# Gate rows six steps earlier, output norm on VectorE alone, and scores led by a pair in the biased attention of a two-layer step

## The reference

```python
h = x * (1 + sc1) + sh1
y = mixer(h)                        # layer 1: grouped-query attention C, then neighbourhood attention D
x = layer_norm(DN_ALPHA * x + gt1 * y, g1, b1)
h = x * (1 + sc2) + sh2
x = layer_norm(DN_ALPHA * x + gt2 * peer_ffn(h), g2, b2)    # layer 1: this is the output y, z

# attention D, for the grid tokens (tiles 1, 2); the prompt tile has plain attention over itself
s_loc = q @ k * scale + bias[head, row offset, column offset]   # 256 local keys
s_loc = where(col_ok, s_loc, -inf)
s_ctx = q @ cached_k * scale                                    # 128 cached keys, no bias
out = softmax(concat(s_loc, s_ctx)) @ concat(v, cached_v)

# peer_ffn: 8 heads pick 16 of 16384 experts per token
out = sum(gate * gelu(u[expert] @ h) * v[expert])
```

## Time and profile before

| | us |
|---|---|
| runs: median (lowest to highest of 3) | 2543.14 (2542.46 to 2548.92) |
| profiled execution | 2539.47 |
| its span, first to last instruction | 2537.70 |
| TensorE busy in the span | 2362.0 (93%) |
| VectorE busy | 1765.0 (70%) |
| ScalarE busy | 772.8 (30%) |
| GpSimd busy | 915.0 (36%) |
| mean granted TensorE clock | 0.970 |

### The profile page before, as it was taken

One profiled execution on the slowest core, in us unless ns is written; L12 is line 12 of the kernel. 1 busy time (PEld: TensorE's weight loads), 2 busy tenths in 40 slices (PEclk: granted clock), 3 DMA queues, 4 the chain that ended last, 5 costly groups with the idle time before them and its releaser, 6 DMA issues.

```text
span 2537.7 us, 34148 instructions
## 1 busy us (share of the span) xinstructions
PE 2362.0 (93%) x12686; PEld 1819.5 (72%) x12686; DVE 1765.0 (70%) x3612; ACT 772.8 (30%) x1388; POOL 915.0 (36%) x650
## 2 busy tenths in 40 slices
PE   5988989999999999999978778999999999999994
PEld 4756789889757866666657467987995777666662
DVE  2335378978669877777644456799785897777775
ACT  2354442113225422222143444311330552222221
POOL 3500361621222265565353205335113124555551
PEclk7999989999999999999989988999999999999997
DMA  7445423986799899999834702279669999999992
GB/s 269 143 167 194 157 100 111 361 325 210 263 340 335 315 397 383 384 388 390 324 114 151 208 28 83 85 277 407 197 206 363 327 331 350 379 389 380 397 380 106
DMA packets 219907, 679.71 MB, mean 268 GB/s; under 512 B 32384, under 2 KB 63152, under 8 KB 219232
## 3 DMA queue, kind: packets, MB, share of 16 engines
q1 hardware_dynamic: 142912, 396.42, 43.7%
q0 software_dynamic: 76832, 281.11, 29.2%
HBM read 658.87 MB, written 18.56 MB: 267 GB/s over the span
## 4 chain that ended last, share of the span: by engine, by line
PE 83%; DMA 6%; DVE 5%; ACT 3%; issue 1%; SPq 1%; POOL 1%; ACTq 0%; DVEq 0%
PE ps L1056 21%; PE ps L1033 15%; PE ps L737 12%; PE ps L738 12%; PE ps L739 12%; DMA ring<-in_u 3%; PE ps L1012 2%; PE ps L900 2%; PE ps L919 2%; DVE v_split L2028 1%; PE ps L987 1%; PE ps L909 1%; PE ps L768 1%; PE ps L760 1%; DMA arena<-in_w_mod 1%
## 5 line engine op out<-in xcount | busy, mean ns | idle before, releaser
L655 POOL DMA_INDIRECT arena<-in_u_rows,arena x256 | 302.5, 1182 | 729.9 <-DVE arena L1844 549.7
L1056 PE MATMUL ps<-ring,arena 128*128 128x512 f32 x1264 | 564.9, 592 | 0.0
L1033 PE MATMUL ps<-arena,ring 128*128 128x256 f32 x2048 | 459.3, 382 | 11.2 <-DMA ring<-in_u 9.9
L655 POOL DMA_INDIRECT arena<-in_v,arena x256 | 354.2, 1384 | 319.2 <-DVE arena L1844 143.3
L1033 PEld LDWEIGHTS ps<-arena,ring 128*128 128x128 f32 x2048 | 384.2, 191 | 69.3 <-issue 18.7
L1056 PEld LDWEIGHTS ps<-ring,arena 128*128 128x128 f32 x1264 | 231.7, 190 | 241.9 <-issue 241.2
L1279 ACT ACTIVATE arena<-ps 128x256 f32<-128x256 f32 x256 | 98.1, 383 | 981.7 <-PE ps L739 618.5
L615 POOL TENSOR_TENSOR ring_lo<-ring,ring_hi 128x1024 fp32r<-128x1024 f32 x84 | 216.1, 2584 | 420.1 <-ACT ring_hi L1158 420.1
L737 PE MATMUL ps<-xs_high,u_split 128*128 128x256 f32 x1024 | 339.0, 331 | 0.0
L2057 DVE SCALAR_TENSOR_TENSOR arena<-arena 128x1024 f32<-128x1024 f32 x254 | 325.6, 1282 | 18.9 <-DMA arena<-in_v,arena 4.3
L1844 DVE CUSTOM_DVE_ANT_0 arena<-arena 128x1024 f32<-128x1024 f32 x256 | 311.0, 1220 | 15.3 <-DMA arena<-in_u_rows,arena 13.9
(11 more groups left out here) (245 smaller groups left out, 3565.2 us busy)
## 6 DMA issues: line engine op xcount, KB each, us to landing
ring<-in_u SPq DMA_DIRECT2D x256, 512.0 KB, 6.6
ring<-in_v SPq DMA_DIRECT2D x256, 512.0 KB, 5.7
ring<-in_w_mod SPq DMA_DIRECT2D x80, 512.0 KB, 4.3
ring<-in_w_in SPq DMA_DIRECT2D x36, 512.0 KB, 3.2
ring<-in_w_q SPq DMA_DIRECT2D x32, 512.0 KB, 3.2
gelu_half<-arena SPq DMA_DIRECT2D x120, 128.0 KB, 4.7
arena<-gelu_half SPq DMA_DIRECT2D x120, 128.0 KB, 4.6
arena<-in_w_mod SPq DMA_DIRECT2D x16, 512.0 KB, 19.5
```

Of the source, the lines that this page charges most:

```text
L655: pool.indirect_dma_start(row[at], None, table, bass.IndirectOffsetOnAxis(where[:, k:k + 1], axis=0)).then_inc(sem(f"row_in{at}"), 16)
L1033: ins = mm(hidden_bank(b), slot[c % RING][:, P * k:P * k + P], HFS[:, k, :], start=(k == 0), stop=(k == KC - 1))
L1056: ins = mm(ps[:, t + 3 * q, :], GL[:, b % GLS, P * t - P:P * t], slot[c % RING][:, 512 * q:512 * q + 512], start=(b == MIDDLE[0]), stop=(b ...
```

## The change

The gate rows go from steps 124-127 to 118-121 on TensorE and ScalarE, in both layers. The norm after the experts no longer waits for the whole last group with tile 1, but for its first four matmuls (a new semaphore). At the end of layer 0 VectorE does its half of tile 0's modulation between tile 1's residual and tile 1's factors; ScalarE does tile 1's normalize ahead of the split of the fourth weight chunk. At the end of layer 1 the whole norm is on VectorE: x minus mean times gain, then times the reciprocal root plus bias; ScalarE only takes the roots, and SyncE stores the tiles.

In the biased attention the bias table gets 384 columns per head, zero over the cached keys, and is held as eight times the bias plus mask, so that one instruction adds it to the raw scores, scales, writes the result and takes the maximum. Scores use four banks and are issued a pair ahead. The mask is added head by head in the last four steps of the attention before.

```diff
+GATE_ROWS = 118
...
+        def score_bank(l, g, i):
+            return (0, 1, 6, 7)[i % 4] if (l, g) == (1, 1) else i % 2
...
@@ SyncE, at its end @@
+            for t in range(NT):
+                sp.wait_ge(sem("y_ready"), t + 1)
+                sp.dma_start(a["y"][P * t:P * t + P, :], Xv[:, t, :]).then_inc(sem("y_out"), 16)
+            sp.wait_ge(sem("y_out"), 16 * NT)
...
@@ GpSimd, at its end @@
-            for t in range(NT - 1):
-                last_bias(t)
-            for t in range(NT):
-                wait_y(pool, t)
-                store(a["y"][P * t:P * t + P, :], Xv[:, t, :], "y_out")
-            pool.wait_ge(sem("y_out"), 16 * NT)
...
@@ TensorE, attention @@
+                lead = 1 if (l, g) == (1, 1) else 0
+                def scores(n):
+                    if n > lead:
+                        pe.wait_ge(sem("p_ready"), since("p_ready", 2 * l + g) + 2 * (n - lead))
+                    for i in (2 * n, 2 * n + 1):
...
+                        mm(ps[:, score_bank(l, g, i), 0:kn], QT[p0:p1, qn, P * t:P * t + P], KT[p0:p1, kt, k0:k0 + kn],
+                           start=True, stop=True).then_inc(sem("sc_ps"), 1)
+                for n in range(lead):
+                    scores(n)
                 for n in range(PAIRS + 2):
...
+                    if n + lead < PAIRS:
+                        scores(n + lead)
...
@@ TensorE, experts @@
+                        if b == KEYS - 1 and t == 1:
+                            ins.then_inc(sem("first_sums"), 1)
...
-                    m = b - KEYS + 4
-                    if m >= 0:
+                    m = b - GATE_ROWS
+                    if 0 <= m < 4:
...
@@ ScalarE @@
-                    m = b - KEYS + 4
-                    if m >= 0:
+                    m = b - GATE_ROWS
+                    if 0 <= m < 4:
                         gate_row(2 * l + 1, m, 0)
-                for c in range(start["uv", l] + 2 * KEYS - RING, start["uv", l] + 2 * KEYS - 2):
-                    done(c)
+                if l == 0:
+                    for c in range(start["uv", l] + 2 * KEYS - RING, start["uv", l] + 2 * KEYS - 2):
+                        done(c)
...
                     feature_half(n + 2, 0)
+                    normalize(n + 1, 1)
                     done(start["uv", l] + 2 * KEYS - 1)
-                    normalize(n + 1, 1)
                     feature_half(n + 2, 1)
...
                 else:
-                    normalize(n + 1, 1)
-                    normalize(n + 1, 2)
+                    for t in range(NT):
+                        deviation(n + 1, t)
...
@@ VectorE, norm @@
-                        if t:
+                        if t == 1:
+                            dve.wait_ge(sem("first_sums"), since("first_sums", n // 2) + 1)
+                        elif t == 2:
                             c = v_chunk(n // 2, KEYS - 1)
...
+                def scaled_rows(t):
+                    x = Xv[:, t, :]
+                    link(stt(x, x, mv[:, 2 * t:2 * t + 1], lnv[:, 0, :], ALU.subtract, ALU.mult))
+                    dve.wait_ge(sem("std"), since("std", n) + t + 1)
+                    link(dve.reciprocal(rstd[:, t:t + 1], rstd[:, t:t + 1]))
+                    stt(x, x, rstd[:, t:t + 1], lnv[:, 1, :], ALU.mult, ALU.add).then_inc(sem("y_ready"), 1)
                 if n < 3:
-                    factors(1)
-                    residual(2)
-                    factors(2)
+                    for t in range(NT):
+                        residual(t)
+                        if n == 1 and t == 1:
+                            features(2, 1)
+                        factors(t)
                 else:
...
+                    for t in range(NT):
+                        residual(t)
+                        dve.wait_ge(sem("var"), since("var", n) + t + 1)
+                        scaled_rows(t)
...
@@ VectorE, attention @@
-                bv = ar(A_BIAS, 4096).rearrange("p (n c) -> p n c", c=64)
-                link(tt(bv, bv, TAB[:, T_MASK:T_MASK + 64].unsqueeze(1).to_broadcast([P, 64, 64]), ALU.add))
+                for t in range(2):
+                    for h in heads:
+                        bv = BIAS[:, t, h, 0:256].rearrange("p (n c) -> p n c", c=64)
+                        ins = stt(bv, bv, 8.0, TAB[:, T_MASK:T_MASK + 64].unsqueeze(1).to_broadcast([P, 4, 64]), ALU.mult,
+                                  ALU.add)
+                link(ins)
...
-                                stt(SC[:, i % 2, 0:256], ps[:, i % 2, 0:256], scale, BIAS[:, t - 1, j, :],
-                                    ALU.mult, ALU.add)
-                                link(ts(SC[:, i % 2, 256:384], ps[:, i % 2, 256:384], scale, None, ALU.mult))
-                            link(dve.tensor_reduce(nm[:, i:i + 1], SC[:, i % 2, :] if in_sb else ps[:, i % 2, 0:kn],
-                                                   AX.X, ALU.max))
+                                link(dve.tensor_tensor_reduce(SC[:, i % 2, :], ps[:, score_bank(l, g, i), 0:TOK], BIAS[:, t - 1, j, :], scale,
+                                                              NEG, ALU.add, ALU.max, nm[:, i:i + 1]))
+                            else:
+                                link(dve.tensor_reduce(nm[:, i:i + 1], ps[:, score_bank(l, g, i), 0:kn], AX.X, ALU.max))
...
-                    if (l, g) == (1, 0) and n == PAIRS:
-                        mask_bias()
+                    if (l, g) == (1, 0):
+                        if n < 2:
+                            dve.memset(BIAS[:, n, :, 256:384], 0.0)
+                        if n >= PAIRS - 2:
+                            mask_bias(range(2 * (n - PAIRS + 2), 2 * (n - PAIRS + 2) + 2))
...
-                features(n)
+                features(n, 0 if l else 2)
```

More of the change, by code:

```diff
@@ L185 @@
     **dict.fromkeys(("h_act", "h_dve", "xhi_act", "xlo_dve", "xlo_pool"), [3, 3, 3, 3]),
-    **dict.fromkeys(("var", "std", "factors", "centred"), [3, 3, 3, 3]),
+    **dict.fromkeys(("var", "std"), [3, 3, 3, 3]),
+    **dict.fromkeys(("factors", "centred"), [3, 3, 3, 0]),
+    **dict.fromkeys(("first_sums",), [1, 1]),
     **dict.fromkeys(("qk_ps",), [8, 16, 5, 8]),
@@ L891, in attention @@
                 pe.wait_ge(sem("qkT_act"), since("qkT_act", 2 * l + g + 1))
-                for n in range(PAIRS + 2):
[L893 to L899, removed]
-                            mm(ps[:, i % 2, 0:kn], QT[p0:p1, qn, P * t:P * t + P], KT[p0:p1, kt, k0:k0 + kn],
-                               start=True, stop=True).then_inc(sem("sc_ps"), 1)
+                lead = 1 if (l, g) == (1, 1) else 0
[3 more added lines that the diff above has]
+                    for i in (2 * n, 2 * n + 1):
+                        j, t = job(l, g, i)
+                        k0, kn = (0, P) if t == 0 else (P, TOK)
+                        p0, p1, qn, kt = place(j)
+                        mm(ps[:, score_bank(l, g, i), 0:kn], QT[p0:p1, qn, P * t:P * t + P], KT[p0:p1, kt, k0:k0 + kn],
+                           start=True, stop=True).then_inc(sem("sc_ps"), 1)
+                for n in range(lead):
+                    scores(n)
+                for n in range(PAIRS + 2):
+                    if n + lead < PAIRS:
+                        scores(n + lead)
                     if 1 <= n <= PAIRS:
@@ L1475, in _ @@
                 experts(l)
-                normalize(n + 1, 0)
                 if l == 0:
+                    normalize(n + 1, 0)
                     done(start["uv", l] + 2 * KEYS - 2)
@@ L1555, in combined, with features @@
                 dve.wait_ge(sem("combined"), n)
-            def features(n):
+            def features(n, begin=2):
                 l, w = n // 2, n % 2
-                dve.wait_ge(sem("mod_ready"), (4, 12, 16, 24)[n])
-                if n:
-                    dve.wait_ge(sem(f"state{(n - 1) // 2}"), 64)
                 def half(t):
+                    if t == 0:
+                        dve.wait_ge(sem("mod_ready"), (4, 12, 16, 24)[n])
+                        if n:
+                            dve.wait_ge(sem(f"state{(n - 1) // 2}"), 64)
                     dve.wait_ge(sem("h_turned"), since("h_turned", n) + 2 * t + 1)
@@ L1576, in low @@
                        ).then_inc(sem("xlo_dve"), 1)
-                half(0)
+                if begin:
+                    half(0)
+                if begin == 1:
+                    return
                 half(1)
@@ L1650, in factors @@
                         ).then_inc(sem("factors"), 1)
-                def gain(t):
-                    dve.wait_ge(sem("centred"), since("centred", n) + t + 1)
-                    tt(Xv[:, t, :], Xv[:, t, :], lnv[:, 0, :], ALU.mult).then_inc(sem("scaled"), 1)
-                residual(0)
-                factors(0)
-                residual(1)
-                if n < 3:
-                    factors(1)
-                    residual(2)
-                    factors(2)
+                def scaled_rows(t):
[4 more added lines that the diff above has]
```

(16 more changed lines are left out.)

20 lines of the change are left out of this document (6 added, 14 removed).

## The result

The change makes the kernel faster: 2503.07 us (median of 4 runs, 2495.72 to 2506.20) against 2545.01 (4 runs of the kernel before on the same chip, 2542.46 to 2548.92). The ratio is 0.983, 95% interval 0.981 to 0.985, or 42 us. The forecast was 32 us saved, 2511, range 2503 to 2524. The direction was right and the saving too small by a quarter: the time lies on the range's lower edge, and the 42 us lie above the 40 that this edge stood for.

A forecast was written before the change was run, and what follows sets the result against it. TensorE, carrying 83% of the chain of waits, was taken as the bound. Savings of 14 + 7.2 + 10.4 + 0.9 - 0.5 = 32.0 us from 2543.1 gave 2511 us, range 2503 to 2524.

The forecast's parts named there:

- Biased attention: Loop of biased attention: joined maximum and scores a pair ahead cut a turn from 11.56 to 8.0 us, 14 us saved.
- rival (b): Biased attention: issuing scores ahead leads nothing, only the shorter maximum counts, 8.8 us; 2516 us, chance 10%.
- Store issue: Kernel's end: last store issued from SyncE's idle queue, up to 1.7 us sooner, 0.9 us taken.
- End of layer 1: Norm after layer 1's experts: VectorE finishes the prompt tile early, last pass ends at 2517.4 against 2527.80, 10.4 us saved.
- End of layer 0: Norm after layer 0's experts: normalizes come earlier, next projection starts 7.2 us earlier, bounds 4 to 9.
- rival (c): End of layer 0 gains nothing: second chunk lands late or tile 1's work blocks its factors; 2518 us, chance 7%.
- Mask: Sixteen mask passes before the biased attention: 0.5 us lost, range from 0.2 gained to 3.2 lost.
- the other case: VectorE keeps its turn between mask passes; last four wait for one GpSimd split, L1534 0.3 to 0.5 us late.
- Gate rows, "this costs nothing": Expert steps 118 to 121, both layers: ScalarE's next split starts about 1.1 us later, without cost; 9 us if cover were gone.
- (a): Half clock in the biased attention loop, TensorE the bound: loses about 4 us instead of gaining 14; 2529 us, chance 8%.
- (d): Clock left at half past the biased attention, into output projection and queries: 13 us slower, 2556 us, chance 2%.
- (e): Whole kernel: everything at its better bound, 37.8 us saved, 2505 us, chance 5%.

## Why the prediction came out as it did

- **Biased attention: turn right, loop mis-sized** (14 forecast, 18.8 measured). The turn was put at 8.0 us and took 8.1, with TensorE idle for 0.8 of it. The step that failed is "The fill and the slow parts, 54.76 - 46.2 = 8.5 us, I leave as they are": they shrank to 35.97 - 4 x 8.1 = 3.6. The loop before had a mean clock of 0.81, so 0.38 x 54.76 = 21 us at half clock; the one after had none. The three slow pieces of the loop before, and then its last piece at full clock, from the run that changed only the stores:

```profile
1452.75:1465.05 12.30, 6.74 (x25) 3.72 (x25) 6.51 (x23) 4.06 (x15) 0.00 (x0) 0.58 0.00 0
1476.61:1489.76 13.15, 9.02 (x54) 6.98 (x54) 7.69 (x29) 5.76 (x19) 0.00 (x0) 0.87 0.00 1
1496.85:1507.51 10.66, 8.08 (x44) 6.92 (x44) 4.46 (x18) 3.43 (x10) 0.00 (x0) 0.68 0.01 2
```

```profile
1504.63:1513.76 9.13, 5.99 (x45) 4.86 (x45) 4.47 (x18) 3.43 (x10) 0.00 (x0) 1.00 0.01 3
```

  The second is a whole turn, 1.6 us over the full-clock 11.56; the third is 1.5 us over the 9.13; the first would take about 10.8 by its pairs (1.9, and two of 4.46), so it is 1.5 us over. Together that is 4.6 us of clock, about what I missed. This is an estimate: it is put together from two runs, and no run held the old loop at full clock. A turn of the new loop with some half clock in it agrees, in the run with the square root moved and in the repeated changed kernel:

```profile
1449.42:1458.35 8.93, 8.91 (x55) 6.83 (x55) 4.55 (x24) 5.53 (x19) 0.00 (x0) 0.81 0.01 2
```

```profile
1459.18:1469.46 10.28, 10.27 (x55) 7.82 (x55) 4.54 (x24) 5.64 (x19) 0.00 (x0) 0.69 0.01 2
```

  That is 0.8 and 2.2 us over 8.1 for 3.4 and 6.4 us at half clock, a quarter to a third; 4.6 for the old loop's 21 is somewhat under a quarter. The price depends on the place: where TensorE waits anyway, half clock can cost nothing. A pair of the old loop took 4.47 us in the run that changed only the stores, at a mean clock of 0.71, and 4.46 at full clock:

```profile
1461.59:1466.06 4.47, 1.29 (x7) 0.51 (x7) 2.58 (x8) 1.47 (x5) 0.00 (x0) 0.71 0.00 0
```

  The sizes of the two parts were also wrong: the joined maximum, 8.8 in rival (b), gave 12.5 alone, of which 4 x 2.5 = 10 lie in the turns.
- **Store issue: mechanism missed** (0.9 forecast, 6.8 measured). The step that failed is "The last store is issued 1.7 us after the addition today (2529.49); from SyncE's idle queue it can be anything from that to at once, and I take 0.9": it asked only for the way to the store and put what stands behind the landing at nothing. The 1.7 did go (0.04 now), and 0.3 of the landing; 4.9 us more were GpSimd's DRAIN, on the path in the kernel before and no longer. Three runs above show it, one of them by GpSimd's release alone.
- **End of layer 1: right** (10.4 and 10.2), the last pass 15.7 us after the last group's start against the 15.6 forecast, and by the forecast's steps: the prompt tile is done 1.1 us after that start (1.1 forecast) and tile 1's residual begins 1.9 us after it (1.9). The run with late gate rows shows that 5.8 of it hang on them.
- **End of layer 0: right** (7.2 and 7.0) by the forecast's steps, each normalize within 0.8 us. The chunk that ScalarE waits for (5.49 us) does stand ahead of the table load, but taking it away gained 0.3, no more than these runs differ by: tile 1's residual could then start 1.8 us earlier, with the half group, and a split took most of that back. So rival (c)'s mechanism is there without its price.
- **Mask: sign right, size between** (-0.5 forecast, -1.6 measured, bound -3.2). The splits did slip in between the passes, the case for which the Trainium skill, SBUF — State Buffer, section "Who interferes with whom", spoke: a VectorE instruction with two SBUF inputs and a GpSimd one that reads SBUF exclude each other. The 7.72 us row agrees. I let the other case decide and should have given this one more weight. The -1.6 of one pair of traces is partly chance: TensorE's wait, which is the mask's own part, grew by 1.4 us there, and over all profiled runs by some 2 (1.9 to 5.0 us, against 1.5 and 2.3).
- **Gate rows, "this costs nothing": right.** From the sums of step 116 to those of step 127 TensorE takes 67.04 us with the rows early and 67.06 with them late, in both layers and in every profiled run. That layer 0's last group starts at 1271.16 and 1271.29 shows nothing here: across the runs this start varies by 12 us.
- **Rivals.** (a) and (d) did not come: in no run of the changed loop did the half clock last more than some 7 us (mean 0.91 over 38.2 us), and there TensorE was busy without a gap. (e), 2505, was nearest to what came by its number alone: it has neither the 6.8 us at the end nor the 18.8 of the loop.
- **Luck in the sum.** By stretches, 32.0 us forecast became 43.8: 4.8 more in the loop, 5.9 at the end, 2.4 in a stretch that no edit touched, and 1.4 less in the rest.
- **Sums that were off without effect.** Rival (a)'s price leaves out the fill: 4 x 14.9 + 8.5 is 13 us over 54.76, not 4. By L1750's row a quarter of its columns takes 1.6 us, not 1.1 (a memset took 0.91). By the working for layer 1 the half-group signal in layer 0 is due at 1273.2, not 1273.6.

## What to carry to other kernels

The end of a program is a stage of its own: read down to its last instruction, DRAINs and all, and ask which engine is released last, before an engine gets the last store. Here both the stores and the bias additions had to leave GpSimd before its DRAIN left the path. A loop with the clock below 1.00 holds a second gain besides the shorter turn (here about 4.6 us, an estimate), and it belongs in the sum, not in the part left as it is. Two edits that open one ring from both ends are not added: alone 12.5 and 10.2 us, together 18.8.

## What the runs showed of the hardware that was not expected

- GpSimd's DRAIN at the end of its program takes 4.89 us (to the nanosecond the same in two kernels) right behind stores of its own, and 9.13 behind a wait alone; SyncE's takes 0.007 us behind its wait for the stores.
- The granted clock fell to 0.5 in the changed loop in some runs (mean 0.81 and 0.69 in one turn, above) and not in others of the same code, so 35.97 us is the loop at its best; the repeated changed kernel took 38.2. A microsecond at half clock cost the loop a quarter to a third of a microsecond in these turns, with TensorE busy without a gap.
